# First mixer of a two-block kernel: gating products among the first attention units, squares in later short units, tiles turned a unit sooner at its end

## The reference, cut to what matters

```python
def spatial_gating(z, ln_g, ln_b, w_s, b_s):
    zu, zv = jnp.split(z, 2, axis=-1)
    zv = layer_norm(zv, ln_g, ln_b)
    zv = zv.reshape(B, nc, SGU_CHUNK, N_SGU_GROUPS, SGU_GROUP_DIM)
    w = w_s * mask[None]
    mixed = jnp.einsum('gij,bcjgd->bcigd', w, zv) + b_s.T[None, None, :, :, None]
    return zu * mixed.reshape(B, S, D_SGU)

attn = forgetting_attention(q, k, v, log_f)   # softmax(q.k/8 + c[t] - c[s]), causal
sgu = spatial_gating(jax.nn.gelu(z), ...)
merged = concatenate([rms_norm(attn, g[:512]), rms_norm(sgu, g[512:])])
x = x + merged @ w_out
```

## Time and profile before

| what | us |
|---|---|
| median of three runs | 2513.77 |
| the runs | 2507.59 to 2515.84 |
| the profiled execution, its time | 2510.12 |
| the profiled execution, its span | 2508.4 |
| PE busy | 2434.0 (97%) |
| DVE busy | 1497.2 (60%) |
| ACT busy | 1051.0 (42%) |
| POOL busy | 1050.1 (42%) |

### The profile page before, as it was taken

One profiled execution on the slowest core, in us unless ns is written; L12 is line 12 of the kernel. 1 busy time (PEld: TensorE's weight loads), 2 busy tenths in 40 slices (PEclk: granted clock), 3 DMA queues, 4 the chain that ended last, 5 costly groups with the idle time before them and its releaser, 6 DMA issues. The chain is left out here.

```text
span 2508.4 us, 35724 instructions
## 1 busy us (share of the span) xinstructions
PE 2434.0 (97%) x13107; PEld 1927.9 (77%) x13107; DVE 1497.2 (60%) x2193; ACT 1051.0 (42%) x2024; POOL 1050.1 (42%) x818
## 2 busy tenths in 40 slices
PE   7999999999999999999999988899999999999998
PEld 6788456878888888887788877764787888888787
DVE  3231653485554567883653245558259888888777
ACT  3200662453333334464233244368255444444444
POOL 4443037165544542332454553253435454443321
PEclk9999999999999999999999999999999999999999
DMA  4110113213322359871111200000411332337985
GB/s 137 47 51 21 51 34 135 101 42 117 110 96 100 120 185 347 283 263 56 47 51 51 55 14 2 7 13 1 168 68 59 121 106 89 110 113 247 333 269 216
DMA packets 165489, 278.30 MB, mean 111 GB/s; under 512 B 16597, under 2 KB 64960, under 8 KB 165320
## 3 DMA queue, kind: packets, MB, share of 16 engines
q1 hardware_dynamic: 160384, 259.15, 30.9%
q10 hardware_dynamic: 4936, 16.90, 1.7%
HBM read 218.81 MB, written 57.18 MB: 110 GB/s over the span
## 5 line engine op out<-in xcount | busy, mean ns | idle before, releaser
L1345 POOL TENSOR_TENSOR ring_lo_conv<-operand_sum_conv,ring_hi_conv 128x512 fp32r<-128x512 f32 x140 | 198.8, 1433 | 260.4 <-ACT ring_hi_conv L1596 260.4
L1345 POOL TENSOR_TENSOR ring_lo<-operand_sum,ring_hi 128x512 fp32r<-128x512 f32 x140 | 190.1, 1368 | 245.0 <-ACT ring_hi L1596 245.0
L115 POOL TENSOR_TENSOR w_hi<-w_raw,zero 128x512 fp32r<-128x512 f32 x92 | 107.0, 1163 | 271.6 <-PE bank L178 199.5
L178 PE MATMUL bank<-xt_hi,w_hi 128*128 128x512 f32 x384 | 149.5, 389 | 0.0
L178 PE MATMUL bank<-xt_hi,w_lo 128*128 128x512 f32 x384 | 149.4, 389 | 0.0
L178 PE MATMUL bank<-xt_lo,w_hi 128*128 128x512 f32 x384 | 149.4, 389 | 0.0
L1469 PE MATMUL bank<-xt_hi,ring_hi_conv 128*128 128x512 f32 x352 | 137.6, 391 | 1.9 <-DVE hidden_raw_conv L1922 1.3
L1469 PE MATMUL bank<-xt_hi,ring_hi 128*128 128x512 f32 x352 | 137.6, 391 | 1.2 <-DVE hidden_raw L1912 0.6
L1471 PE MATMUL bank<-xt_hi,ring_lo_conv 128*128 128x512 f32 x352 | 137.0, 389 | 0.0
L1471 PE MATMUL bank<-xt_hi,ring_lo 128*128 128x512 f32 x352 | 137.0, 389 | 0.0
L1470 PE MATMUL bank<-xt_lo,ring_hi_conv 128*128 128x512 f32 x352 | 137.0, 389 | 0.0
(11 more groups left out here) (601 smaller groups left out, 6798.4 us busy)
## 6 DMA issues: line engine op xcount, KB each, us to landing
down_in<-in_w_down_dram SPq DMA_DIRECT2D x130, 256.0 KB, 4.7
down_in_conv<-in_w_ffn_down_dram SPq DMA_DIRECT2D x130, 256.0 KB, 4.7
up_raw<-in_w_gate_up_dram SPq DMA_DIRECT2D x88, 256.0 KB, 3.7
up_raw_conv<-in_w_ffn_up_dram SPq DMA_DIRECT2D x88, 256.0 KB, 3.7
down_in<-hidden_between SPq DMA_DIRECT2D x76, 256.0 KB, 3.9
down_in_conv<-hidden_between_conv SPq DMA_DIRECT2D x76, 256.0 KB, 3.9
w_raw<-in_w_mix_in_dram SPq DMA_DIRECT2D x64, 256.0 KB, 2.7
hidden_between<-hidden_sums SPq DMA_DIRECT2D x11, 1024.0 KB, 4.3
```

The lines of the kernel that those rows point to most:

```text
L115: pool.tensor_tensor(m.w_hi[:, u, :], m.w_raw[:, u, :], zeros, ALU.add).then_inc(m.hi_done, 1)
L178: mm = pe.matmul(m.psum[b][:, :], lhs, rhs, start=k == 0 and i == 0, stop=k == KD - 1 and i == 2)
L1345: pool.tensor_tensor(shaped(ring_lo[SLOT[e]][:, :], e), source(e), shaped(ring_hi[SLOT[e]][:, :].bitcast(F32), e), ALU.subtract).then_inc( ...
```

## The change

PE: gating products 0 and 1 stand ahead of `scores(0)`, product 2 between `scores(0)` and `scores(1)`, and products 3 to 7 behind the turns of units 0, 1 and 2, in banks 6 and 7 alone. DVE's gates follow the same order. The wait for all eight gates moves from the first turn to the first value product, and, on ACT, from unit 0 to the first square. The squares stand behind units 5, 6, 7, 13, 14, 15, 21 and 22. At the end, the value products of half head 6 stand in three slots instead of five; groups 0 to 3 of `sgu_turn`, with their high and low parts, stand in unit 30 instead of behind it (PE) and behind unit 31 (ACT, DVE); the spreading of half head 6 stands behind them; `inverse(7)` stands ahead of `out(6)`; ACT's `high(6)` stands behind all eight gating high parts.

```diff
--- before.py
+++ after.py
@@ -532,8 +532,11 @@
 
         return (0, 1) if units[u][1] >= 4 else (u % 2,)
 
+    GATING_SLOTS = ((0, 0), (0, 1), (1, 1), (2, 0), (2, 1))
+    SQUARES = (5, 6, 7, 13, 14, 15, 21, 22)
     VALUE_SLOTS = ((0, 1), (1, 0), (1, 1), (2, 0), (2, 1))
     VALUE_PARTS = ((0, 1, 2, 3, 4, 4), (0, 2, 3, 5, 6, 8))
+    END_SLOTS, END_PARTS = ((0, 1), (1, 0), (1, 1)), (0, 3, 5, 8)
     pieces = [(u, a, c) for u in range(NU) for c in banks_of(u) for a in range(2)]
     at_piece = {x: n for n, x in enumerate(pieces)}
     groups = [(u, a, g) for u in range(NU) for a in range(2) for g in range(1 + units[u][1] // 4)]
@@ -609,8 +612,6 @@
                         pe.wait_ge(pta, copied(n - 2, "act"))
                     else:
                         pe.wait_ge(ptd, copied(n - 2, "dve"))
-                else:
-                    pe.wait_ge(sgu_out, 8)
                 for j in range(4 * g, min(i + 1, 4 * g + 4)):
                     mm = pe.transpose(m.psum[4 + n % 2][:, (j % 4) * P:(j % 4 + 1) * P],
                                       sc[:, u % 3, a, j * P:(j + 1) * P], m.ident[:, :])
@@ -626,8 +627,11 @@
                     pe.wait_ge(ptd, copied(last, "dve"))
                 if hh:
                     pe.wait_ge(attn_out, hh)
+                else:
+                    pe.wait_ge(sgu_out, 8)
             nj = 4 + 4 * high
-            for j in range(VALUE_PARTS[high][part], VALUE_PARTS[high][part + 1]):
+            parts = END_PARTS if hh == 6 else VALUE_PARTS[high]
+            for j in range(parts[part], parts[part + 1]):
                 c0 = max(0, j - 4 * high) * P
                 for a in range(2):
                     mm = pe.matmul(m.psum[6][64 * a:64 * a + 64, c0:HALF],
@@ -658,26 +662,34 @@
                 mm = pe.transpose(m.psum[n % 4][:, j * P:(j + 1) * P], zu[:, 4 * h + j, k * P:(k + 1) * P], m.ident[:, :])
             mm.then_inc(s_turn, 1)
 
-        for g in range(8):
-            if g >= 4:
-                pe.wait_ge(sgu_out, g - 3)
-            if g == 4:
-                scores(0)
-            pe.matmul(m.psum[4 + g % 4][:, :], w_sT[:, g, :], zv[:, :, g * 64:(g + 1) * 64],
+        def gating(g):
+            if g >= 2:
+                pe.wait_ge(sgu_out, g - 1)
+            pe.matmul(m.psum[6 + g % 2][:, :], w_sT[:, g, :], zv[:, :, g * 64:(g + 1) * 64],
                       start=True, stop=True).then_inc(sgu, 1)
+
+        gating(0)
+        gating(1)
+        scores(0)
+        gating(2)
         scores(1)
         for u in range(NU):
             for a in range(2):
                 turn(u, a)
                 if a == 0 and u + 2 < NU:
                     scores(u + 2)
-                if u >= 4 and (u % 4, a) in VALUE_SLOTS:
-                    values(u // 4 - 1, VALUE_SLOTS.index((u % 4, a)))
-                    if (u % 4, a) == VALUE_SLOTS[-1]:
+                if (u, a) in GATING_SLOTS:
+                    gating(3 + GATING_SLOTS.index((u, a)))
+                slots = END_SLOTS if u >= LAST else VALUE_SLOTS
+                if u >= 4 and (u % 4, a) in slots:
+                    values(u // 4 - 1, slots.index((u % 4, a)))
+                    if u < LAST and (u % 4, a) == slots[-1]:
                         spread_rows(u // 4 - 1)
+                if u == LAST + 2:
+                    sgu_turn(2 * a)
+                    sgu_turn(2 * a + 1)
             if u == LAST + 2:
-                for n in range(4):
-                    sgu_turn(n)
+                spread_rows(6)
         for n in range(4, 8):
             sgu_turn(n)
         for part in range(len(VALUE_SLOTS)):
@@ -713,7 +725,7 @@
         def sgu_gate(g):
             dve.wait_ge(sgu, g + 1)
             dve.scalar_tensor_tensor(zu[:, :, g * 64:(g + 1) * 64],
-                                     m.psum[4 + g % 4][:, :].rearrange("p (c d) -> p c d", c=NT),
+                                     m.psum[6 + g % 2][:, :].rearrange("p (c d) -> p c d", c=NT),
                                      m.cols[:, ROW["b_s"] + g:ROW["b_s"] + g + 1],
                                      zu[:, :, g * 64:(g + 1) * 64], ALU.add, ALU.mult).then_inc(sgu_out, 1)
 
@@ -770,25 +782,29 @@
                                      m.xt_hi[:, 4 + k, tok].bitcast(F32), ALU.mult, ALU.subtract).then_inc(s_lo, 1)
 
         dve.memset(ones[:, :], 1.0).then_inc(start, 1)
-        for g in range(4):
-            sgu_gate(g)
+        sgu_gate(0)
+        sgu_gate(1)
         score(0)
-        for g in range(4, 8):
-            sgu_gate(g)
+        sgu_gate(2)
         score(1)
         for u in range(NU):
             copies(u, 0)
             if u + 2 < NU:
                 score(u + 2)
+            if (u, 0) in GATING_SLOTS:
+                sgu_gate(3 + GATING_SLOTS.index((u, 0)))
             if u % 4 == 0 and u:
                 inverse(u // 4 - 1)
             copies(u, 1)
+            if (u, 1) in GATING_SLOTS:
+                sgu_gate(3 + GATING_SLOTS.index((u, 1)))
+            if u == LAST + 2:
+                for n in range(4):
+                    sgu_low(n)
+            if u == LAST + 3:
+                inverse(NU // 4 - 1)
             if u % 4 == 3 and u > 4:
                 out(u // 4 - 1)
-            if u == LAST + 3:
-                for n in range(4):
-                    sgu_low(n)
-        inverse(NU // 4 - 1)
         for n in range(4, 8):
             sgu_low(n)
         out(NU // 4 - 1)
@@ -843,23 +859,23 @@
                 if u + 1 < NU:
                     exps(u + 1, a)
                 copies(u, a)
-                if u % 4 == 3 and u > 4 and a == 0:
+                if u == LAST + 2:
+                    sgu_high(2 * a)
+                    sgu_high(2 * a + 1)
+                if u % 4 == 3 and u > 4 and a == (1 if u > LAST else 0):
                     spread(u // 4 - 1)
                 if u % 4 == 0 and u > 4 and a == 0:
                     high(u // 4 - 2)
-            if u == 0:
-                act.wait_ge(sgu_out, 8)
-            if u in (1, 2, 3, 5, 6, 7, 9, 10):
-                t = (1, 2, 3, 5, 6, 7, 9, 10).index(u)
+            if u in SQUARES:
+                t = SQUARES.index(u)
                 if t:
                     act.wait_ge(s_ss, t)
+                else:
+                    act.wait_ge(sgu_out, 8)
                 act.activation(junk[:, :], zu[:, t, :], ACT.Square, accum_out=ss[:, 1, t:t + 1]).then_inc(s_ss, 1)
-            if u == LAST + 3:
-                for n in range(4):
-                    sgu_high(n)
-                high(NU // 4 - 2)
         for n in range(4, 8):
             sgu_high(n)
+        high(NU // 4 - 2)
         spread(NU // 4 - 1)
         high(NU // 4 - 1)
```

## The result

The kernel before took 2512.36 us (median of 20 runs, 2507.53 to 2516.16), the changed one **2515.94 us** (median of 20, 2508.35 to 2518.73). The ratio is **1.0015, 95% interval 1.0008 to 1.0022**: 3.8 us slower, between 2.0 and 5.5. The profiled execution of the changed kernel took 2513.8 us, its span is 2512.1, 3.7 longer than before.

A forecast was written before the change was run, and what follows sets the result against it. PE, busy 2434.0 of 2508.4 us, was taken as the bound. The sums' start, opening included, gave -0.1 us and the clock +1.0, so +0.9 on a mean of 2511.8: 2512.7 us, range 2507 to 2518.

The forecast's parts named there:

- clock term behind the sums: After PE's new wait before the sums, 1 to 3.4 us of low clock would slow the dense products: +1.0 us.
- part 1: Opening, units 0 to 3: moved gating products fill PE's idle but add waits for DVE; -0.2 us, bounds -1.3 and +1.5.
- which the change doesn't move: Opening: the landing of gate_rows holds DVE's first scores until 259.27, before and after the change alike.
- lower bound of -1.3: Opening's best case: waits for DVE's banks are hidden, leaving 2.56 us less the wait for the DMA.
- Rival (d): Opening does the reverse, +1.5 us with DVE late, the rest as forecast: +2.4 us in all; chance 0.04.
- The squares: Moving eight ACT squares from units 1, 2, 3, 9 and 10 to short units: worth 0.0, costing nothing.
- PE is 3.6 us sooner here: End of the mixer stage: the next stage's first product starts at about 399.0 instead of 402.59.
- The closed POOL chain: Before the sums: POOL works without a stop from 397.26 to 412.94, leaving PE 0.46 us of slack.
- POOL's operation of L902: POOL's operation at 397.26, waiting for ACT's high part of half head 6, would start 0.5 us later.
- rival (b): Before the sums: POOL's chain starts later still, by another 1.5 us, with a clock cost: +3.2 us; chance 0.13.
- Rival (c): The end's gap is won and the idle of units 0 to 3 filled: -3.6 - 2.56 = -6.2 us; chance 0.06.

The follow-up runs named there:

- e7: The kernel before with POOL's three split slices of w_out moved behind half head 7, nothing else; ratio 0.9994 (0.9982 to 1.0005) to the kernel before.
- e2: The changed kernel with the opening and the squares put back as before, so only the new end; ratio 1.0009 (1.0000 to 1.0019) to the kernel before.
- e8: The changed kernel with the first two gate_rows loads issued at the end of the stage before; ratio 0.9999 (0.9990 to 1.0009) to the kernel before.
- e10: The changed kernel again, unaltered, timed beside other runs of the kernel before; ratio 1.0013 (1.0002 to 1.0024).
- e11: The kernel before with only the eight squares moved to their new units; ratio 1.0002 (0.9993 to 1.0011).
- e6: The changed kernel with old opening and squares, and POOL's three split slices moved behind half head 7; ratio 0.9988 (0.9978 to 0.9999) to the kernel before.
- e1: The changed kernel with the end put back, so only new opening and squares; ratio 1.0005 (0.9996 to 1.0013) to the kernel before.
- e9: The changed kernel with early gate_rows loads and POOL's split slices behind half head 7; median 2502.67 us, ratio 0.9971 (0.9961 to 0.9981) to the kernel before.
- e13: The kernel before with the first two gate_rows loads issued at the end of the stage before; ratio 1.0002 (0.9991 to 1.0013).
- e4: The changed kernel with 15 unused products filling PE's wait before the sums; ratio 1.0009 (1.0000 to 1.0019) to the kernel before.
- e12: The changed kernel with early gate_rows loads and 15 unused products in PE's wait before the sums; ratio 0.9990 (0.9980 to 1.0001) to the kernel before.
- e3: The changed kernel with POOL's three split slices of w_out moved behind half head 7; ratio 0.9990 (0.9981 to 0.9999) to the kernel before.

## Why the prediction was right or wrong

**The time was in the range, the sum was not.** I had +0.9 us, measured +3.8 (2.0 to 5.5). That 2515.94 lies between 2507 and 2518 says little, as the range was mostly the scatter of single executions. The step that failed first of all is the size of the clock term behind the sums: put at 1.0 us, measured at 3.2. The second is part 1, put at -0.2, measured at +1.18 in one execution and -0.08 in another.

**The landing of gate_rows (part 1).** The mechanism was right: PE waits for a bank that DVE frees, DVE waits for the DMA, and that eats what the moved products win. The step that failed is that I took 259.27 in the earlier trace rows as fixed, "which the change doesn't move". It varies: over the profiles with the loads in their old place DVE started 5.05 to 7.02 us after the first product. Nor is it shown that the change leaves it alone. The five profiles with the old opening have 5.05 to 5.59, the five with the new one 5.59 to 7.02 (5.95 and 5.59 for the changed kernel itself), though the loads are issued at the same point. So part of the later landing may come with the new order; no run tests that. The old opening hides a landing up to about 5.2 (unit 4 at 26.32 with 5.05, 26.58 with 5.44 in e7, 26.72 with 5.59 in e2), for PE had more products to do; the new one hands every tenth on: unit 4 at 23.81 with the first score at 3.15 (e8), at 26.24 with 5.59 (e10), 2.43 later for 2.44. In the changed kernel it was 5.95, so 0.36 of the 1.26 us to e10 is the landing. PE's wait, which I had at 1.3 and 0.4, was 2.31 here, and 1.95 and 0.21 in e10. And I priced no clock in the opening: with 2.31 us of idle it fell (0.62, 0.50, 0.50, 0.67), with 1.95 in e10 it didn't, which leaves 0.9 for the fall. So the term was -0.2 and measured +1.18 and, in e10, -0.08. By the same count, as an estimate, a landing at 5.05 without a fall would have given unit 4 at 25.70, that is -0.6: of the +1.18, 0.9 is the later landing and 0.9 the fall. The lower bound of -1.3 kept the wait for the DMA; with the landing out of the way the term is -2.5 (e8). That isn't the idle of the earlier trace rows alone: a wait of 0.67 before unit 4, which I had read as 0.45, stays, so 1.9 us is idle won, and 0.6 is PE being busy for less time up to that turn (23.13 us against 23.74, both at full clock), which no run explains. Rival (d) had part 1 reversed because DVE would be late with its gates; in the changed kernel's profile part 1 was reversed, but by the landing and the clock.

**The squares.** 0.0 forecast, 0.0 measured (e11).

**The end up to the next stage.** "PE is 3.6 us sooner here": counted from unit 4 it is 4.4 (3.20 + 1.18 in the changed kernel, 4.41 in e6). The mechanism was right, the idle of 2.28 us is gone and the clock holds at 1.00 to 402.6; the size was 0.8 short. Counted from unit 4 and put on the times of the earlier trace rows, PE began the last four `sgu_turn` at 392.9, where I had 393.7. Half of that is the turns of unit 31, which had ended by 393.33 before the change and which I counted once more; the other half may be the value products of half head 6, whose rows take 6.25 us in three slots and 6.70 in five, but no run separates that. Of the 4.4, 1.2 is the clock: e1, with the old end and no fall there, needed 21.60 us for the stretch for which the kernel before needed 22.84. That the next stage began at 398.93, where I had 399.0, is luck: the 0.8 was eaten by a unit 4 that came 0.7 later.

**POOL's chain.** "The closed POOL chain" catches the gain: PE's new idle before the sums was forecast at 3.6 and is 3.49. A small part of the step was wrong in sign: I had POOL's operation of L902 0.5 later. It came 17.36 us after the turn of unit 28 against 17.51 before, 0.15 sooner, as ACT's high parts followed PE's earlier turns. The sums followed the end of POOL's last sum after 0.11 us, where it had been 0.68 (412.94 to 413.62 before). In all they came 0.7 sooner, counted from unit 4, where I had 0.1 later. Hence rival (b), POOL's chain late by more than 0.46 us, didn't happen, though its +3.2 stands near the measured value; the chain itself took 15.66 us (15.68 before).

**The clock behind the sums: the term that failed.** I had 1 to 3.4 us at 1.2 GHz, cost 1.0. The fall came where I had put it, in the sums after the idle, but it lasted from 414 to 422: 0.16 + 6 + 0.66 = 6.8 us low, at a cost of 3.23. I had taken the 3.4 us of the earlier trace rows as the longest that a fall lasts, and thought part of it would lie under the sums. Neither held: the sums themselves took 2.43 instead of 1.84, and everything behind them is dense. Term by term, the ledger has +1.18 where I had -0.2, -0.72 where I had +0.1, and +3.23 where I had +1.0; in e10 it has -0.08, -0.74 and +3.24. Without the falls of the clock, that of the opening (0.9) and that behind the sums, both executions would come out faster than before, by 0.4 and 0.8 us. The Trainium skill (TensorE: Matmul & The Clock Gate, "Part 1: The HAM clock gate") says of the ramp, the slow products before the full clock is granted, that its penalty is "<1% of a typical kernel span". The traces agree for a fall in mid-kernel, as 3.2 of 2512 us is 0.13%. But the measured loss was 0.15%, so here the small term decided the sign.

**Rival (c), the whole gain.** I gave it -6.2 us and named the two things against it. Both were the right ones: e9 takes away exactly these two and measures -7.3 (-9.8 to -4.8), in the ledger -6.9.

**What scattered.** Over the 20 runs of the changed kernel the time falls by 1.8 us for each 0.001 of mean granted clock (correlation -0.91; 2508.35 us at 0.997, 2518.73 at 0.992), over 35 runs of the kernel before, in each of three sets, by 1.6 to 2.0 (about -0.8). The mean clock was 0.9941 for the changed kernel and 0.9953 to 0.9957 for the kernel before in the three later sets: 0.0012 to 0.0016, or 2.2 to 2.9 of the 3.8 us. Beside runs of its own set, e10 had 0.9947 against 0.9957. That the slope is causal is argued, not shown; it is near what a microsecond at 1.2 GHz costs, as 0.001 of the mean is 5 us at half speed, which do the work of 2.5.

## What to carry to other kernels

Before a wait of the busiest engine is filled, ask which chain of another engine stands next, how much slack it leaves (0.46 us here) and what can be moved out of that chain: the same edit was +2.3 us without and -3.0 us with the splitting of three slices moved. An operand that lands "just in time" in one profile may land 1 or 2 us later in the next, so take work away from in front of it only when its load is issued sooner. And where effects are of a thousandth, price the clock after each new idle, at both places where it can fall, from a second execution if there is one.

## What the runs showed of the hardware

The length of a fall took two values: over the 14 profiles there are 15 falls in this stretch, and each lasted 3.4 or 6.8 us. It was 3.4 after 2.28 us of idle at the end of the stage (before, e7, e11, e13), after 2.31, 2.45 and 3.09 us in the opening (the changed kernel, e1, e4), after 0.51 us before the sums (e1), and behind filled idle (e4, e12). It was 6.8 after 3.48 to 3.50 us before the sums (the changed kernel, e2, e8, e10) and after 3.39 us in the opening (e3). After 1.95 us in the opening (e10) there was none. The landing of the same loads, issued at the same point, varied by 1.4 us between executions with the same opening, and by 2 over both openings. And a gap of 2.28 us lowered the clock at the end of the stage in before (0.82, 0.50) and not at all in e1, whose stage has the same end with the same 2.28 us of wait. Its one-microsecond stretches, beside the earlier trace rows:

```profile
396.00:397.00 1.00, 0.39 (x4) 0.39 (x4) 1.00 (x2) 1.00 (x3) 0.97 (x1) 1.00 1.04 334
397.00:398.00 1.00, 1.00 (x8) 0.52 (x7) 1.00 (x3) 1.00 (x3) 0.00 (x0) 1.00 0.84 272
```

PE starts again at 396.6 and stays at 1.00, where the kernel before fell to 0.50 within two microseconds. So the same idle costs 1.2 us more or less from one execution to the next (22.84 and 21.6 us from the turn of unit 28 to the next stage), and no run here tells what decides it. The four profiles with the old end that fell there (before, e7, e11, e13) held the clock at the sums; e1, which held it there, fell at the sums.
